# Two heads' scores issued together, the first stage by token blocks, one branch around the overflow loop

## What is computed

```python
h = rmsnorm(x, g);  proj = h @ w_in
A: score = sum_h relu(q_idx[h] @ k_idx) * w_idx[h]      # 4 index heads of depth 32
   sel = top 256 keys by score;  softmax(qa @ ka / 8, on sel) @ va        # depth 64
B: mLSTM, in blocks of tokens
C: softmax(qc @ kc / 8 + bias, on a band of up to 640 keys) @ vc          # depth 64
D: (softmax(q0 @ k0) - lam * softmax(q1 @ k1)) @ vd                       # two maps of depth 32
x = x + (sum_n sigmoid(h @ w_gate)[n] * (y_n @ w_branch[n])) @ w_out
x = x + mixture of experts(rmsnorm(x));  return rmsnorm(x, g_final)
```

## Time and profile before

| what | us |
|---|---|
| median of 3 runs | 2068.76 |
| runs, lowest and highest | 2065.22, 2073.78 |
| the profiled execution | 2076.17 |
| its span, first to last instruction | 2074.1 |
| PE busy in it | 1860.3 (90%) |
| DVE busy | 1400.9 (68%) |
| ACT busy | 909.1 (44%) |
| POOL busy | 222.7 (11%) |
| mean granted clock of PE, share of full speed | 0.930 |

### The profile page before, as it was taken

How to read it: one execution, slowest core, us unless ns; L and a number is a source line. 1 busy time by engine, 2 the same in 40 slices (tenths; PEclk the granted TensorE clock), 3 DMA queues, 4 the chain that set the end, 5 groups by cost and what they waited for, 6 DMA issues and landing times. The chain is left out here.

```text
span 2074.1 us, 24448 instructions
## 1 busy us (share of the span) xinstructions
PE 1860.3 (90%) x8818; PEld 1408.0 (68%) x8818; DVE 1400.9 (68%) x1874; ACT 909.1 (44%) x1135; POOL 222.7 (11%) x164
## 2 busy tenths in 40 slices
PE   4999999698999999999998897964999999999970
PEld 4757888577777776777676776753777777777740
DVE  4366959868988888531121664236999999999956
ACT  5423211112334433333333542012777787777742
POOL 0000000013000012000000331000222221121103
PEclk9999999857999999999999898976999999999985
DMA  4101122100243422131210662044999999999926
GB/s 161 61 1 61 56 87 92 37 0 26 66 172 123 127 80 61 62 102 61 82 61 34 222 232 115 37 186 180 350 396 396 398 399 399 402 400 399 406 85 253
DMA packets 75642, 356.11 MB, mean 172 GB/s; under 512 B 8648, under 2 KB 11208, under 8 KB 49192
## 3 DMA queue, kind: packets, MB, share of 16 engines
q1 hardware_dynamic: 66088, 321.45, 41.6%
q0 software_dynamic: 5888, 20.97, 3.1%
q10 hardware_dynamic: 3584, 12.58, 1.5%
HBM read 299.01 MB, written 55.97 MB: 171 GB/s over the span
## 5 line engine op out<-in xcount | busy, mean ns | idle before, releaser
L2135 DVE TENSOR_TENSOR wa_lo<-wa,w_hi 128x2048 fp32r<-128x2048 f32 x128 | 289.8, 2286 | 15.5 <-ACT w_hi L2048 14.1
L2048 ACT ACTIVATE w_hi<-wa 128x2048 fp32r<-128x2048 f32 x128 | 244.6, 1915 | 63.0 <-PE psum L1993 36.4
L1315 PE MATMUL psum<-h_hi,w_hi 128*128 128x512 f32 x512 | 228.5, 446 | 2.1 <-ACT gate_out L963 1.9
L1315 PE MATMUL psum<-h_hi,w_lo 128*128 128x512 f32 x512 | 203.4, 397 | 0.0
L1315 PE MATMUL psum<-h_lo,w_hi 128*128 128x512 f32 x512 | 202.6, 396 | 0.0
L167 DVE MAX8 top<-sel 128x8 f32<-128x384 f32 (+5 forms) x192 | 171.4, 893 | 4.6
L1977 PE MATMUL psum<-w_hi,xT_hi 128*96 128x512 f32 x512 | 164.7, 403 | 5.1 <-DVE wa_lo L2135 5.1
L165 DVE MATCH_REPLACE8 sel<-top,sel 128x384 f32<-128x384 f32 (+5 forms) x192 | 168.1, 876 | 0.0
L2142 DVE TENSOR_TENSOR wb_lo<-wd,w_hi 128x2048 fp32r<-128x2048 f32 x64 | 143.9, 2288 | 34.7 <-ACT w_hi L2057 34.7
L1977 PE MATMUL psum<-wa_lo,xT_hi 128*96 128x512 f32 x512 | 160.7, 395 | 0.0
L1977 PE MATMUL psum<-w_hi,xT_lo 128*96 128x512 f32 x512 | 160.6, 395 | 0.0
(11 more groups left out here) (359 smaller groups left out, 3541.5 us busy)
## 6 DMA issues: line engine op xcount, KB each, us to landing
wa<-expert_up SPq DMA_DIRECT2D x128, 1024.0 KB, 10.4
wd<-expert_down SPq DMA_DIRECT2D x64, 1024.0 KB, 10.9
w<-w_gate SPq DMA_DIRECT2D x32, 512.0 KB, 4.2
gate_pre<-gate_out SPq DMA_DIRECT2D x64, 256.0 KB, 3.6
gate<-gate_pre SPq DMA_DIRECT2D x32, 512.0 KB, 4.9
ys<-yo ACTq DMA_DIRECT2D x32, 384.0 KB, 7.0
w<-w_T SPq DMA_DIRECT2D x18, 512.0 KB, 3.7
ys<-zeros SPq DMA_DIRECT2D x7, 1152.0 KB, 5.9
```

What stands on the lines that cost most here:

```text
L1315: ins = nc.tensor.matmul(psum[:, 7, :], w[:, k, :], x[:, k, half * 512:(half + 1) * 512], start=(n == 0), stop=(n == BURST - 1))
L2048: nc.scalar.activation(hi_a(j, q).rearrange("p c m n -> p (c m n)"), wa[j][q][:, :, :, :].rearrange("p c m n -> p (c m n)"), ACT.Copy).the ...
L2135: nc.vector.tensor_tensor(wa_lo[j][q][:, :, :, :].rearrange("p c m n -> p (c m n)"), wa[j][q][:, :, :, :].rearrange("p c m n -> p (c m n)" ...
```

## The change

Three parts. **The first stage** goes by token blocks: for each block square, root, scale with the gain (now a full row `gain1` in SBUF, loaded to all partitions, in place of `gT`), eight transposes in two steps (`turn`), taking out and rest, and the 268 columns into banks 4 to 7; engines run these steps of different blocks beside each other. The loads are reordered, the Sigmoid of `oB` is one instruction over all blocks at the end. **Scores of two heads** are issued in one call, chunk by chunk in turn: for the index scores with 16 value matmuls after each pair, and for C and A at every even unit, for units what + 2 and what + 3. D still takes one unit at a time, its two maps now in turn by chunk. **The overflow loop** stands inside one branch on blocks > 0.

```diff
@@ sync
+            for t in range(NT):
+                sp.dma_start(xs[:, t, :], a["x"][t * P:(t + 1) * P, :]).then_inc(x_in[t], 16)
+                if t == 0:
+                    sp.dma_start(gain[:, :], a["g_mix"].partition_broadcast(P)).then_inc(gain_in, 16)
+                if t == 1:
+                    sp.dma_start(w12[:, :, :], a["w_gates12"]).then_inc(w12_in, 16)
...
@@ scalar
+            act.wait_ge(eps_ready, 1)
+            for t in range(NT + 4):
+                if t < NT:
+                    act.wait_ge(x_in[t], 16)
+                    nc.scalar.activation(relu[t % 2][:, :], xs[:, t, :], ACT.Square,
+                                         accum_out=ssq[:, t:t + 1]).then_inc(squared, 1)
                     act.wait_ge(squared, t + 1)
+                    nc.scalar.activation(rstd[:, t:t + 1], ssq[:, t:t + 1], ACT.Sqrt, bias=eps[:, 0:1],
+                                         scale=1.0 / DM).then_inc(root_ready, 1)
+                if t == 1:
+                    act.wait_ge(w12_in, 16)
...
+                if 2 <= t < NT + 2:
+                    h_out(t - 2)
...
+                if t >= 4:
+                    tok_out(t - 4)
...
+            act.wait_ge(tok_taken, NT)
+            nc.scalar.activation(s.oB[:, :, :], s.oB[:, :, :], ACT.Sigmoid)
@@ vector
+            for t in range(NT + 2):
+                if t < NT:
+                    dve.wait_ge(root_ready, t + 1)
+                    link(nc.vector.reciprocal(rstd[:, t:t + 1], rstd[:, t:t + 1]))
+                    nc.vector.scalar_tensor_tensor(out=xs[:, t, :], in0=xs[:, t, :], scalar=rstd[:, t:t + 1],
+                                                   in1=gain[:, :], op0=ALU.mult, op1=ALU.mult).then_inc(normed, 1)
...
+                if t >= 2:
+                    h_rest(t - 2)
@@ tensor
+            turn(0)
             for t in range(NT):
+                if t + 1 < NT:
+                    turn(t + 1)
                 if t == 0:
-                    pe.wait_ge(h_low, 2 * KC)
+                    pe.wait_ge(w12_low, 2)
+                pe.wait_ge(h_low, 2 * t + 2)
                 if t >= 4:
                     pe.wait_ge(tok_taken, t - 3)
-                tok_part(t, GW, w12_hi, w12_lo, 0, 3 * KC)
+                tok_part(t, 4 + t % 4, GW, w12_hi, w12_lo, 0, 3 * KC)
...
-                for h in range(NH):
+                for h in range(0, NH, 2):
                     if n >= 2:
-                        pe.wait_ge(idx_taken, n - 1)
+                        pe.wait_ge(idx_taken, n)
                     for c0 in range(0, wd, 512):
                         c1 = min(wd, c0 + 512)
...
+                        for g in range(2):
+                            row = DI * (h + g)
+                            ins = nc.tensor.matmul(psum[:, 4 + 2 * g + c0 // 512, 0:c1 - c0],
+                                                   idx_qk[row:row + DI, 0, b * P:(b + 1) * P],
+                                                   idx_qk[row:row + DI, 1, c0:c1], start=True, stop=True)
+                            if c1 == wd:
+                                ins.then_inc(idx_ready, 1)
...
+                    for part in range(n, n + 2):
...
@@ attend, tensor
+            def score(first, count):
...
+                places = [(u, r, slot) for u in range(first, first + count) for r, slot in enumerate(slots(u))]
+                for c0 in range(0, nk * P, 512):
+                    c1 = min(nk * P, c0 + 512)
+                    for u, r, slot in places:
+                        h, prev = units[u][2], before(u, slots)
+                        if c0 == 0 and prev is not None:
...
+                                pe.wait_ge(stats_ready, n_exp[prev + 1])
...
-                    ahead = min(what + (1 if kind == "D" else 2), NU - 1)
-                    for u in range(scored + 1, ahead + 1):
-                        score(u)
-                    scored = max(scored, ahead)
+                    if what + 1 < NB:
+                        score(what + 1, 1)
+                    elif what + 1 == NB:
+                        score(NB, 2)
+                    elif what % 2 == 0 and what + 2 < NU:
+                        score(what + 2, 2)
@@ experts, overflow
-        with eng.Fori(0, N_OV) as b:
-            with eng.If(blocks > b):
+        with eng.If(blocks > 0):
+            with eng.Fori(0, N_OV) as b:
                 body(b)
```

More of the change, by code:

```diff
@@ L362, in _ @@
[L362 to L384, removed]
+            def h_out(t):
+                for q in range(2):
+                    act.wait_ge(xT_ready, 2 * t + q + 1)
+                    nc.scalar.activation(s.h_hi[:, 4 * q:4 * q + 4, t * P:(t + 1) * P],
+                                         psum[:, (2 * t + q) % 4, :].rearrange("p (c n) -> p c n", n=P),
+                                         ACT.Copy).then_inc(h_high, 1)
@@ L496, in silu @@
                 dve.wait_ge(conv_done, n + 1)
[L498 to L522, removed]
+            def h_rest(t):
+                for q in range(2):
+                    dve.wait_ge(h_high, 2 * t + q + 1)
+                    toks = slice(t * P, (t + 1) * P)
+                    nc.vector.tensor_tensor(s.h_lo[:, 4 * q:4 * q + 4, toks],
+                                            psum[:, (2 * t + q) % 4, :].rearrange("p (c n) -> p c n", n=P),
+                                            s.h_hi[:, 4 * q:4 * q + 4, toks].bitcast(F32),
+                                            ALU.subtract).then_inc(h_low, 1)
@@ L523, in _ @@
+            dve.wait_ge(small_in, 32)
             s.split_low(dve, 0)
@@ L586, in _, with tok_part @@
             pe.wait_ge(ident_ready, 2)
[L588 to L593, removed]
-                    ins = nc.tensor.transpose(psum[:, n % 4, t * P:(t + 1) * P],
-                                              xs[:, 4 * h + t, c * P:(c + 1) * P], s.ident[:, :])
-                ins.then_inc(xT_ready, 1)
-            def tok_part(n, cols, w_hi, w_lo, first, count):
+            def tok_part(n, bank, cols, w_hi, w_lo, first, count):
                 t = n % NT
@@ L1259, in _ @@
                 ins.then_inc(b_pv, 1)
[L1262 to L1264 removed]
+            def score(first, count):
+                kind, b, h = units[first]
+                k0, nk = keys(kind, b)
+                if first == NB:
                     pe.wait_ge(c_in, 48)
[L1266 removed]
+                if first == 2 * NB:
                     pe.wait_ge(a_in, 48)
[L1268 to L1277 removed]
+                places = [(u, r, slot) for u in range(first, first + count) for r, slot in enumerate(slots(u))]
[4 more added lines that the diff above has]
+                        if c0 == 0 and prev is not None:
+                            if units[prev][0] == "D":
+                                pe.wait_ge(exp_done, n_exp[prev] + (r + 1 if kind == "D" else 2))
+                            else:
+                                pe.wait_ge(stats_ready, n_exp[prev + 1])
@@ L1278, in score @@
                         if kind == "D":
-                            row = DI * (2 * (h % 2) + r)
-                            q = s.q2[row:row + DI, h // 2, b * P:(b + 1) * P]
-                            k = s.k2[row:row + DI, h // 2, c0:c1]
-                        else:
-                            q = head(q_of[kind], h, b, 1)
-                            k = k_of[kind][HD * (h % 2):HD * (h % 2) + HD, h // 2, k0 * P + c0:k0 * P + c1]
-                        ins = nc.tensor.matmul(psum[:, 2 * slot + c0 // 512, 0:c1 - c0], q, k, start=True, stop=True)
@@ L1286, in score @@
-                    ins.then_inc(scores_ready, 1)
+                            row, rows = DI * (2 * (h % 2) + r), DI
+                        else:
+                            row, rows = HD * (h % 2), HD
+                        ins = nc.tensor.matmul(psum[:, 2 * slot + c0 // 512, 0:c1 - c0],
+                                               q_of[kind][row:row + rows, h // 2, b * P:(b + 1) * P],
+                                               k_of[kind][row:row + rows, h // 2, k0 * P + c0:k0 * P + c1],
+                                               start=True, stop=True)
@@ L1321, in _ @@
             pe.wait_ge(b_normed, NT)
-            score(0)
-            scored = 0
+            score(0, 1)
             waiting, weighed = [], [0]
```

90 lines of the change are left out of this document (46 added, 44 removed).

## The result

The changed kernel took **1981.11 us**, the median of four runs (1980.05 to 1982.95), against 2067.45 for four runs of the kernel before beside it. The ratio is 0.9569, 95% interval 0.9552 to 0.9586. The prediction was 1985 with a range of 1973 to 2002 and 0.98 for faster: sign and time were right, and the range held. Against the median of 2068.76 that the prediction started from, the gain is 87.7; it said 83.8.

The account below looks back on a forecast made before the run. PE bounds the kernel, busy nine tenths or more of nearly every slice. Terms 13 + 18.5 + 40 + 12.3 = 83.8 us take the profiled run from 2076.17 to 1992.4 and the median from 2068.76 to 1985, range 1973 to 2002.

Parts of the forecast that it names:

- First stage, 13 foretold: First stage: PE no longer waits for all eight blocks; columns start at 15.5, end at 50.5 against 63.9, 13 us less.
- the 2.5 for a slow start and lockstep: First stage: 2.5 us added to its end of 48.0 for a slower clock at the start and lockstep waits.
- Index scores, 18.5 foretold: Index stage: paired heads on different array rows overlap, 12 of 24 scorings go; 18.5 us less, bounds 15 and 19.5.
- the 0.5 taken off for ACT: Index stage: 0.5 us taken off the 19 because ACT holds back the second Relu in four pairs.
- C and A, 40 foretold: C and A scores: paired units overlap, 19.2 and 22.4 less, minus 1.6 of small waits; 40 us, bounds 35 and 42.
- the new wait for the extremes: C and A, even units: also waits for unit what + 1; scored over 7 us earlier, DVE needs under 4 us.
- D, 0: D: its two maps already overlap through both chunks, so no gain, 0 us.
- Rival 4: D: program order holds, so D gains too, 14 us over 16 wide units, 1971; chance 0.03.
- Overflow, 12.3 foretold: Overflow loop: 21 passes on five engines go, ACT arrives last; 12.3 us less, bounds 11.7 to 12.5.
- Lockstep or a late load in the first stage: First stage: ends at 54 us or later, 3 to 8 us given back, 1988 to 1993; chance 0.09.
- Heads that don't overlap: Index heads, or heads of over 128 columns, don't overlap; only the outer parts stay, 2043; chance 0.05.
- The clock at half in C and A: C and A: less PE work halves the granted clock, 314 us would double, 2299, slower; chance 0.01.

Follow-up runs that it names:

- select_in_idx: Changed kernel with 15 more DVE selection half steps in the index stage and 15 fewer beside the last two weight tiles; 1971.63 us.
- head_by_head: Changed kernel with pairs and D units issuing all chunks of the first head (map), then all of the second; 1981.74 us.
- same_rows: Changed kernel with each pair's second head in index stage, C and A reading the first head's operands in the same array rows; 2024.52 us.
- loop_bare: Changed kernel with the overflow loop without the branch around it, the branch back inside each pass; 1994.16 us.

## Why the prediction was right, by its own steps

**First stage, 13 foretold, 16.5 found.** The 268 columns began at 16.7 and not at 15.5, 1.2 late: `w12` landed at 10.3 and not at 9, as the loads moved 315 to 328 GB/s from 3 to 6 us where the prediction took 418 throughout. ACT's split of `w12` began then, 1.2 behind the 9.1 of the prediction. The two loads of an activation table (1.28 each), which the prediction left out at this place, had held ACT until 10.0 and hid behind that. The first 13 matmuls then took 0.223 us each, 2.9 us in all, where the later ones take 0.124; this is the pace of the lower level, 1.2 GHz, as the last section shows. From there the sum was too careful: the 24 matmuls take 24 x 0.124 = 3.0 us a block, not the 3.2 read from a stretch with a dip in it; the transposes 0.79 and not 1.0, and those of six blocks and not of seven stand in the stretch, since block 1's come ahead of the first columns (the x16 at 10.34); and of the 2.5 for a slow start and lockstep only the 1.3 of the slow matmuls came. PE is the longest engine of this stage as foretold, and ACT waits for it block by block. The Sigmoid over 2048 columns with its table load (1.28 + 1.92, ending at 51.1) is hidden: the distance from the gate transposes to the index scores is 24.87 in both traces.

**Index scores, 18.5 foretold, 20.7 found,** which is above the upper bound of 19.5. At full clock 19.1 are left, as 19 was the sum ahead of the 0.5 taken off for ACT; the rest is a dip in the trace of before, which is luck. That 0.5 was not needed: the cadence at width 1024 is 5.78, where two heads took 7.92. DVE's waits for ACT's Relus were the 18.7 us of the earlier trace rows and a second line that the prediction didn't show, 30.4 us together; they fell to 9.3. Before, then after:

```profile
DVE sel L557 <- ACT relu L416: 11.7, 5, 2.7
```

```profile
DVE sel L565 <- ACT relu L424: 6.1, 5, 1.5
DVE sel L567 <- ACT relu L424: 3.2, 2, 2.0
```

This slack paid for the shorter stage, as the prediction had it, and select_in_idx shows that some is left.

**C and A, 40 foretold, 41.7 found.** The mechanism and the sum by widths held: A has 21.6 of its 22.4. C has 20.1 of 19.2, but only by the half clock that went, which is luck; the scores alone brought 17, 2 too few. One place of the missing is seen: at the second pair the new wait for the extremes cuts the call in two (it begins at 731.87) and costs 0.59, once in the stage. The prediction had held that DVE would always be in time for it.

```profile
732.95 0.48 PE L1301 MATMUL psum<-k,q 64*128 64x128 f32 x2 [0.59 <-DVE stat L1179]
```

**D, 0.** 272.97 against 272.32. Rival 4 is denied by this and by head_by_head.

**Overflow, 12.3 foretold, 12.6 found.** ACT is last, and takes 0.9 us from reading the count and not 1.1. The one jump over the whole body takes 0.05 us on ACT and 0.25 on PE, under the 0.72 that the prediction allowed for it. The 12.6 lie 0.1 above the term's upper bound.

**From the trace to the median.** The prediction carried the distance between trace and median over to the new kernel (1992.4 against 1985). It was not carried over: the trace after lies 1.1 below its median. The trace lost 12.4 more than the sum said: 7.7 in the stages that the terms are of, 4.7 in the others, mostly the mixing. A part of that is chance: in the second trace of before the mixing begins after a gap of 8.7 us and not 10.1, and its first product takes 100.3 and not 102.4. Against the 12.4 stand the 7.4 + 1.1 = 8.5 by which the two traces lie apart from their medians. So the small miss in the median, 3.9, is the difference of two larger errors.

One reading was off: the runs of before don't lie within 4 us of their median, the highest is 5.0 above it.

**The other rivals.** Lockstep or a late load in the first stage: only the 1.2 us of the late load. Heads that don't overlap: denied by the records. same_rows shows that this rival's price was wrong too: it takes 2024.5 and not 2043, as the rival left out what fewer calls save with no overlap (4.9 in the index stage, 12.4 in C and A). The clock at half in C and A: it got better, not worse.

## What to carry to other kernels

Price a score call as a fixed part and a part by width before you price its overlap: here a third of what pairing brought in C and A (12.4 of 38.5 us, the dip left out) came from making fewer calls, and would have come with no overlap at all. Two heads on different rows of the array overlapped here when they were issued in one call, whichever way their chunks were ordered. When DVE work is moved off the critical path, move it to a stretch where the trace shows DVE waiting (17.16 us in one piece), not to one where its mean is low: 20 half steps moved there brought 11 us, and moved to C nothing.

## What the runs showed of the hardware

- A branch takes 0.21 to 0.25 us on PE's queue and 0.045 to 0.063 on the others (medians in before, after and loop_bare), and an empty pass of the loop 0.75 us on PE against 0.43 on ACT. So the empty loop was dearest on PE, the engine that bounds this kernel.
- The first 13 matmuls of the first stage came every 0.223 us while the granted clock in the profile says 1.00, and later ones every 0.124 us:

```profile
16.70:19.60 2.90, 2.90 (x13) 2.90 (x14) 2.87 (x5) 1.69 (x4) 0.52 (x1) 1.00 1.02 392
21.90:24.90 3.00, 3.00 (x27) 3.00 (x26) 1.70 (x5) 2.64 (x7) 1.20 (x2) 1.00 0.37 156
```

  In loop_bare, the same code at the same place, they come every 0.125 us up to 17.4 and then every 0.223 us at a granted clock of 0.50, both beside the same transfers (DMA share 1.0):

```profile
16.88:17.38 0.50, 0.50 (x5) 0.50 (x5) 0.50 (x1) 0.50 (x2) 0.00 (x0) 1.00 1.09 377
17.61:20.50 2.89, 2.89 (x15) 2.89 (x15) 2.85 (x5) 0.75 (x3) 1.39 (x1) 0.50 1.01 400
```

  So 0.223 us is the pace of the lower level, 1.2 GHz, and not a matter of the loads; the granted clock of the changed kernel's trace doesn't show that stretch.

- A pair of heads of 64 rows overlaps almost fully at every width seen: 1.35 for two against 1.34 for one at 640 keys, 1.99 against 1.98 at 1024.
